# Re-ordering the seams of a two-block transformer kernel: weight splits on GpSimd, matmuls of one half first, modulation segments hosted elsewhere

## The reference, cut to what matters

```python
def ada_norm(x, g, shift, scale):
    return rms_norm(x, g) * (1.0 + scale) + shift

def swiglu(h, w_in, w_out):
    a, b = jnp.split(h @ w_in, 2, axis=-1)
    return (jax.nn.silu(a) * b) @ w_out

for l in range(DEPTH):
    mx = (s_lat @ ada_w[l] + ada_b[l]).reshape(bsz, N_MOD, 1, d)
    x = x + 0.5 * mx[:, 2] * swiglu(ada_norm(x, norm_g[l, 0], mx[:, 0], mx[:, 1]), ffn_w_in[l, 0], ffn_w_out[l, 0])
    hx = ada_norm(x, norm_g[l, 1], mx[:, 3], mx[:, 4])
    ...   # even or odd mixer on hx (and the context), giving yx
    x = x + mx[:, 5] * yx
    x = x + 0.5 * mx[:, 8] * swiglu(ada_norm(x, norm_g[l, 2], mx[:, 6], mx[:, 7]), ffn_w_in[l, 1], ffn_w_out[l, 1])
```

## Time and profile before

| quantity | value |
|---|---|
| median of 3 runs | 2415.8 us (2412.93 to 2417.66) |
| the profiled execution's own time | 2415.8 us |
| its span, first to last instruction | 2414.0 us |
| TensorE matmul busy | 2302.7 us, 95% |
| VectorE, ScalarE, GpSimd busy | 1156.8, 855.3, 154.4 us |
| mean granted TensorE clock | 0.978 |

### The profile page before, as it was taken

How to read it: one execution, slowest core, us unless ns; L and a number is a source line. 1 busy time by engine, 2 the same in 40 slices (tenths; PEclk the granted TensorE clock), 3 DMA queues, 4 the chain that set the end, 5 groups by cost and what they waited for, 6 DMA issues and landing times.

```text
span 2414.0 us, 36092 instructions
## 1 busy us (share of the span) xinstructions
PE 2302.7 (95%) x13748; PEld 1881.9 (78%) x13748; DVE 1156.8 (48%) x1955; ACT 855.3 (35%) x1388; POOL 154.4 (6%) x137
## 2 busy tenths in 40 slices
PE   6999999999999999978899999999999999988998
PEld 4777797877777788856787777788888876967998
DVE  5226375643433444475553333354343345566665
ACT  4125454632212232246432222233222234355544
POOL 0003112100000010040100000010000010000000
PEclk8999999999999999998999999999999998998999
DMA  9653543445555354300355665343243232323574
GB/s 299 195 161 95 166 139 87 145 127 172 180 179 175 89 146 140 114 10 27 96 154 149 189 188 149 111 123 88 70 118 90 79 104 70 88 70 113 164 205 119
DMA packets 514693, 313.01 MB, mean 130 GB/s; under 512 B 15899, under 2 KB 513138, under 8 KB 514454
## 3 DMA queue, kind: packets, MB, share of 16 engines
q1 hardware_dynamic: 513992, 311.33, 44.1%
q10 hardware_dynamic: 590, 0.16, 0.0%
HBM read 310.41 MB, written 1.05 MB: 129 GB/s over the span
## 4 chain that ended last, share of the span: by engine, by line
PE 85%; DVE 8%; ACT 3%; issue 2%; DMA 1%; ACTq 0%; POOL 0%; DVEq 0%; POOLq 0%
PE ps L1033 64%; PE ps L1075 4%; PE ps L768 4%; PE ps L982 2%; DVE w_lo L1814 2%; ACT w_hi L1351 1%; PE ps L2067 1%; PE ps L952 1%; PE ps L910 1%; PE ps L2388 1%; PE ps L2046 1%; PE ps L879 1%; PE ps L2054 1%; PE ps L841 1%; PE ps L2368 1%
## 5 line engine op out<-in xcount | busy, mean ns | idle before, releaser
L1033 PE MATMUL ps<-h_hi,w_hi 128*128 128x512 f32 (+1 forms) x2096 | 758.4, 362 | 20.7 <-DVE w_lo L1814 9.0
L1033 PE MATMUL ps<-h_hi,w_lo 128*128 128x512 f32 (+1 forms) x2096 | 746.2, 356 | 0.0
L1033 PE MATMUL ps<-h_lo,w_hi 128*128 128x512 f32 (+1 forms) x2096 | 746.2, 356 | 0.0
L1033 PEld LDWEIGHTS ps<-h_hi,w_hi 128*128 128x128 f32 x2096 | 397.9, 190 | 109.9 <-issue 36.8
L1814 DVE TENSOR_TENSOR w_lo<-stage,w_hi 128x1024 fp32r<-128x1024 f32 x227 | 283.2, 1250 | 393.5 <-ACT w_hi L1351 393.2
L1033 PEld LDWEIGHTS ps<-h_hi,w_lo 128*128 128x128 f32 x2096 | 398.3, 190 | 62.4
L1033 PEld LDWEIGHTS ps<-h_lo,w_hi 128*128 128x128 f32 x2096 | 398.4, 190 | 58.7
L1351 ACT ACTIVATE w_hi<-stage 128x1024 fp32r<-128x1024 f32 x227 | 236.7, 1055 | 364.8 <-PE ps L1033 251.0
L1814 DVE TENSOR_TENSOR w_lo<-deep,w_hi 128x1024 fp32r<-128x1024 f32 x184 | 224.9, 1232 | 266.7 <-ACT w_hi L1351 265.7
L1351 ACT ACTIVATE w_hi<-deep 128x1024 fp32r<-128x1024 f32 x184 | 190.7, 1054 | 171.0 <-PE ps L1033 121.0
L1033 PE MATMUL ps<-g_hi,w_hi 128*128 128x512 f32 (+1 forms) x660 | 242.6, 368 | 0.5 <-DVE w_lo L1814 0.2
(11 more groups left out here) (404 smaller groups left out, 2825.9 us busy)
## 6 DMA issues: line engine op xcount, KB each, us to landing
modw<-in_ada_w SPq DMA_DIRECT2D x72, 1024.0 KB, 6.1
stage<-in_ffn_w_in SPq DMA_DIRECT2D x88, 512.0 KB, 4.9
deep<-in_ffn_w_in SPq DMA_DIRECT2D x88, 512.0 KB, 4.0
modw<-in_w_mod SPq DMA_DIRECT2D x18, 1024.0 KB, 7.8
stage<-in_w_in SPq DMA_DIRECT2D x30, 512.0 KB, 4.8
stage<-in_ffn_w_out SPq DMA_DIRECT2D x32, 384.0 KB, 3.5
stage<-in_even_w_in SPq DMA_DIRECT2D x24, 512.0 KB, 4.0
deep<-in_ffn_w_out SPq DMA_DIRECT2D x32, 384.0 KB, 3.6
```

Source lines behind the costliest of these rows:

```text
L1033: last = mm(ps[:, j, 0:b - a], w_part[wp][:, u % RING, c, :], x_part[xp][:, x, a:b], start=first and wp == xp, stop=final and wp == "lo")
```

## The change

It has five parts.

1. Seams A and B host no modulation segments any more (`segs` is gone, in the plan and in all engines' code). The four segments go to the two gemms at L301 and L305, which follow seam A; each of them now hosts four segments (`hper=4`) and not two.
2. TensorE's order `behind` for v=0 becomes (0,0) to (0,4), then (1,0), (0,5), (1,1), (0,6), (1,2), (0,7), then (1,3) to (1,7). The sums of the second half move to after (0,5), its `pe_half_rstd` to after (0,7).
3. GpSimd makes two of the w_lo tiles in each seam: u0+5 and u0+7 in A and C, with its second `add` between them, and u0+4 and u0+5 in B, with the second `add` behind both. DVE makes u0+4 as before and u0+6 ahead of chunk 5's `low` in A and C, and none in B between the chunks. DVE waits on `w_ready` there, so that the count keeps its order.
4. ACT's splits are spread: one each ahead of `high` of chunks 0, 1, 2 and 3 in A and C, and ahead of chunks 1 and 3 in B. Its root for the second half comes behind all eight `high`.
5. On DVE `low` of chunk c now stands ahead of `scaled` of chunk c+1 for v=0, and the diagonal of the second half comes behind all eight chunks.

```diff
-            seam(tail, w, (0, 1), dst=0, segs=2)
+            seam(tail, w, (0, 1), dst=0)
...
-            gemm(w, 512, 4, "copy", dst=4, hper=2)
+            gemm(w, 512, 4, "copy", dst=4, hper=4)
...
-            gemm(w, 1536, 4, "copy", dst=8, hper=2)
+            gemm(w, 1536, 4, "copy", dst=8, hper=4)
...
-            behind = [(q, n) for ns in (chunks[:2], chunks[2:3], *([n] for n in chunks[3:])) for q in range(2) for n in ns]
+            behind = [(0, n) for n in chunks[:5]] + [(q, n + 5 * (1 - q)) for n in chunks[:3] for q in (1, 0)] + [(1, n) for n in chunks[3:]]
...
-            return ((4,), (5, 6), (7,)) if len(p.kw["ks"]) == 2 else ((), (4,), (5,))
+            return (((4,), (5,), (6,), (7,)), (5, 7)) if len(p.kw["ks"]) == 2 else (((), (4,), (), (5,)), (4, 5))
...
             for c in range(KC):
-                for s in seam_splits(p)[c] if c < 3 else ():
-                    dve_split(eng, u0 + s)
+                if c == 0 and per == 2:
+                    dve_split(eng, u0 + 4)
+                if c == 5 and per == 2:
+                    eng.wait_ge(S("w_ready"), u0 + 6)
+                    dve_split(eng, u0 + 6)
                 if c in (0, 2):
                     evacuate(1, c // 2)
+                low(0, c)
                 if c + 1 < KC:
                     scaled(0, c + 1)
-                low(0, c)
-                if c == 6:
-                    dve_half_diag(eng, p, 1, 2)
+            dve_half_diag(eng, p, 1, 2)
             scaled(1, 0)
...
+            def split(u):
+                eng.wait_ge(S("w_hi"), u + 1)
+                eng.wait_ge(S("w_ready"), u)
+                up(nc.gpsimd.tensor_tensor(w_lo[:, u % RING], arrival(u)[0], w_hi[:, u % RING].bitcast(F32), ALU.subtract), "w_ready")
+
             add(0)
-            add(1)
+            split(u0 + first)
+            if first == 5:
+                add(1)
+            split(u0 + second)
+            if first == 4:
+                add(1)
```

More of the change, by code:

```diff
@@ L247, in plan, with seam @@
         last = l == DEPTH - 1
-        def seam(tail, start, norm, dst=None, segs=0):
+        def seam(tail, start, norm, dst=None):
             units = 2 * len(tail["ks"]) + 4
@@ L254, in seam @@
                 r.update({"x_done": 4, "sg_half": 4, "gh_hi": 4, "g_half": 2, "g_ready": 2})
[L255 to L259, removed]
+            add("seam", r, start=start, norm=norm, dst=dst, **tail)
         def ffn(i, nt, hpers, after=None):
@@ L316, in plan @@
             gemm(("even_w_out_2", 0), 0, KC - 2, "resid", sumsq="early", **tail)
-            seam(dict(w=("even_w_out_2", 0), **tail), ("ffn_w_in_2", 0, 1), (0, 2), segs=2)
+            seam(dict(w=("even_w_out_2", 0), **tail), ("ffn_w_in_2", 0, 1), (0, 2))
         else:
@@ L987, in pe_seam @@
                         up(last, "unit_done", by=2) if v else up(last, "x_done")
[L988 to L992, removed]
+                    if v == 0 and (q, n) == (0, 5):
                         early_sums(1)
                         sums(1)
-                    if v == 0 and (q, n) == (1, 5):
+                    if v == 0 and (q, n) == (0, 7):
                         pe_half_rstd(eng, p, 1, 2)
@@ L1302, in act_seam @@
             for c in range(KC):
-                for s in seam_splits(p)[c] if c < 3 else ():
-                    act_split(eng, u0 + s)
+                if c < 4:
+                    for s in seam_splits(p)[0][c]:
+                        act_split(eng, u0 + s)
                 high(0, c)
@@ L1752, in dve_seam @@
             for c in range(KC):
-                for s in seam_splits(p)[c] if c < 3 else ():
-                    dve_split(eng, u0 + s)
+                if c == 0 and per == 2:
[3 more added lines that the diff above has]
+                    dve_split(eng, u0 + 6)
                 if c in (0, 2):
                     evacuate(1, c // 2)
+                low(0, c)
                 if c + 1 < KC:
                     scaled(0, c + 1)
-                low(0, c)
-                if c == 6:
-                    dve_half_diag(eng, p, 1, 2)
+            dve_half_diag(eng, p, 1, 2)
             scaled(1, 0)
-            if k["segs"]:
-                dve_rows(eng, p, 0, 2, 1, 1)
             for c in range(KC):
@@ L1770, in dve_seam @@
                     gated(0, c // 7)
-                if c == 5 and k["segs"]:
-                    dve_cols(eng, p, 0, 2, 1, 1)
+            eng.wait_ge(S("w_ready"), u1 + 4)
             dve_split(eng, u1 + 4)
@@ L1929, in pool_seam @@
         def pool_seam(eng, p):
+            u0 = p.at("unit_done")
+            first, second = seam_splits(p)[1]
             def add(v):
```

4 lines of the change are left out of this document (1 added, 3 removed).

## The result

The changed kernel takes 2442.07 us (median of 4 runs, 2437.34 to 2444.86), the kernel before 2416.73 us beside it: a ratio of 1.0105, 95% interval 1.0085 to 1.0127, or 20 to 31 us more. The forecast was 2437 us, range 2423 to 2447. Slower is right, and the time is 5 us above the likeliest value.

A forecast was written before the change was run, and what follows sets the result against it. TensorE was taken as the bound, its matmuls filling 95% of the span. Seams 13.3, moved segments 5.3 and clock 2.5 us sum to +21.1 us on 2415.8: 2437 us, range 2423 to 2447.

The forecast's parts named there:

- the sum of the seams: New parts of seams A, B and C together: +13.3 us from the layouts, and 2.5 for the clock.
- The chunk cycle: DVE and ACT in v=0 of the seams: 1.44 us per chunk, TensorE waiting about 0.74 us for chunks 1 to 4.
- GpSimd's split: One w_lo tile of 1024 columns on GpSimd in the seams takes 2.40 us, bounds 1.29 and 3.61.
- Blocking: In the seams DVE's low waits until GpSimd's split ends; seams cost 13.3 us with this, 5.0 without.
- Rival 1: GpSimd and DVE don't block each other in the seams: seams +5.0 us, total 2426 us; chance 0.20.
- Seam A: New part +3.9 us: tile 7's late DMA and GpSimd's split delay the chunks, w_lo 7 coming after 12.8 us.
- Seam B: New part +4.1 us: GpSimd's tiles 4 and 5 block low of chunks 1 and 3.
- Seam C: New part +5.3 us: v=0 ends 5.9 later, waiting for GpSimd's tile 7; the second wait shrinks by 0.7.
- Clock: TensorE, partly idle, drops to the 1.2 GHz level in all three seams: +2.5 us, bounds 0 and 7.
- The segments: Gemms behind seam A: four moved segments at 1.1 us plus 0.1 refill, two transpose pairs at 0.25: +5.3 us.
- Rival 2 (collision): Segment DMAs collide in gemms with four segments: plus 3 to 6 us on 2437, 2441 us; chance 0.13.
- Rival 3 (faster): h_lo 1 to 4 run ahead of TensorE, leaving no wait in the new parts: -7.6 us, 2408 us; chance 0.03.

The follow-up runs named there:

- order_only: Changed kernel with all undone but TensorE's v=0 order, the places of sums and roots, and the spread of ACT's and DVE's splits: 1.0019 times the kernel before.
- gpsimd_only: Kernel before with only GpSimd's two splits per seam, their waits and DVE's tile 6 as in the changed kernel: 1.0050 times the kernel before.
- gates_late: Kernel before with silu and gated of the first tile pair behind chunk 7, not 4, in v=1 of seams B and C: 0.9977 times before.
- low_first_only: Kernel before with only DVE's low of chunk c put ahead of scaled of chunk c+1 in v=0: 0.9994 times the kernel before.
- pool_one_input: Changed kernel with GpSimd's two splits per seam made one-input instructions (w_hi times zero), leaving out those tiles' low part: 2429.78 us, one run.
- segs_moved_only: Kernel before with only the four segments moved from seams A and B into the two gemms behind seam A: 1.0025 times the kernel before.
- dve_splits: Changed kernel with GpSimd's two splits per seam given back to DVE, low still ahead of scaled: 1.0060 times the kernel before.
- scaled_ahead: Changed kernel with DVE's scaled of chunk c+1 again ahead of low of chunk c in v=0: 1.0073 times the kernel before.

## Why the prediction was right, step by step

The pair of profiled executions is 29.85 us apart. The new parts have 15.05 of it, the two gemms with four segments 6.26, the old parts ahead of them -0.72. The other 9.3 lie where the change moves nothing: 2.96 before seam A, 2.7 between the two gemms and seam B, 3.6 behind seam C (there the changed kernel's matmuls run at the slower of two rates, shown in the last section). order_only has 2.0 and 4.4 us at the last two places, though its instructions there are those of before; gpsimd_only and gates_late start seam A earlier than before. The prediction had no term for this spread; by medians the kernel is 25.3 us slower, and the terms that can be placed give 20.6, just inside the interval of 20 to 31.

The mechanism was right: the signs that the prediction named are in the trace, but for two in seam A, its longest wait (below) and its length of 35.25 us for about 33. That the sum of the seams came out so close (15.05 against 15.8) is partly luck. The layouts had `low` freed too late, which made seams B and C 1.5 and 1.0 us too long, and the term for the clock was too small by 2.1.

- **The chunk cycle, 1.44 us**: measured 1.45 (1643.91 to 1645.36). TensorE's steps for chunks 3 and 4 of seam A start 1.45 us apart too (897.78 and 899.23); the trace shows 0.49 us of it as idle where 0.74 was told, since it counts a matmul as busy beyond the start of the next. low_first_only shows for the old order what the prediction says of chunks 5 to 7: with two steps of TensorE per chunk the cycle is covered. It costs only under the new order.
- **GpSimd's split, 2.40 us**: 2.38.
- **Blocking**: `low` at 2.31 us beside it. Rival 1 (no blocking, 2426 us) falls by this row. But the prediction's price for blocking, 8.3 us (13.3 less 5.0), is not shown: pool_one_input, with almost none, has seams only 3.3 us shorter than the changed kernel. Its GpSimd instructions are 0.4 us longer and its clock in C is lower, so the 3.3 is no exact price either.
- **Seam A, +3.9**: +5.32. Tile 7 is ready 12.7 us after the part's start, as laid out (12.8). From there to the end it is 22.5 us, not 20.2. TensorE is busy throughout that stretch, at a clock of 0.86: the missing 2.3 us are put down to the clock, which no experiment changed by itself. TensorE's longest wait in A is not where the prediction had it: it stands before chunk 3 (3.15 us), and the wait for GpSimd's tile 7 is 1.60.
- **Seam B, +4.1**: +3.99, with two errors that cancel. The longest wait stands before chunk 3 as told, 2.48 us. But h_lo 3 is ready 7.3 us after the start, 1.5 earlier than laid out (8.85), mostly since `low` of chunk 3 did not have to wait for GpSimd's `add`. From there to v=1 it is 12.7 us and not 11.1, with a low clock in it that the layout did not have (0.79):

```profile
1231.40:1239.40 8.00, 7.16 (x46) 6.96 (x47) 4.39 (x11) 2.29 (x5) 0.88 (x2) 0.79 0.63 197
```

- **Seam C, +5.3**: +5.74. Tile 7 comes 10.5 us after the start, 1.0 earlier than laid out, because the blocked `low` got its turn before GpSimd's `add` did (rows above: `low` ends at 1640.88, `add` takes 0.93 and not 0.74). The 22.7 us behind it, at a clock of 0.92, were laid out as 21.2.
- **Clock, +2.5**: what lies over the layouts behind the last late tile or chunk is 2.3 us in A, 1.6 in B and 1.5 in C, 5.4 in all. Of this the prediction took 0.8 as the slow stretch that seam A had before, so the term comes to 4.6, an estimate from these three differences. It was sized too small.
- **The segments, +5.3**: 6.26. The term that was too small is the transposes: 0.25 us a pair counts no wait, as in a gemm with two segments, where DVE's sum is long done. With four, the transposes of the first pair follow the rows at once and wait 0.55 us, and transposes and wait together cost 0.9 a pair.
- **Rival 2 (collision)**: SP does hold the third and fourth segments back (12.77 us for the two DMAs in its queue), but no wait of TensorE for modw follows.
- **Rival 3 (faster)**: no part of the change, alone or with others, was faster than before by more than can be measured.

Each part alone gives 6.0 (segments), 12.1 (GpSimd), -1.5 (low first, not clear of zero) and 4.6 us (order with spread), 21.2 in all; the whole gives 25.3, and its interval reaches down to 20. So the totals prove no effect of the parts on each other.

What stays open: whether the 25.3 us of the medians exceed the 20.6 that have a place at all, whether scaled ahead of low is worth 3 or 8 us, what the blocking is worth in seams A and C, and what holds `low` for 0.5 us beside a one-input instruction.

## What to carry to other kernels

A helper engine that takes work off a busy one can be paid for twice, if it is slower at it (2.38 against 1.22 us here) and shuts the other out meanwhile (2.31 us for a `low` of 0.48): look at whether the next instruction of the relieved engine has the operands that collide, and at when the helper's last piece is needed. An order in which the consumer asks for one input per step needs the producers' cycle at or below the step; the same cycle is free if the consumer alternates with work that it already has. Before work is moved out of a place that looks crowded, check whether the new place has idle time: a filler that hides half its cost in waits pays all of it in a dense loop.

## What the runs showed of the hardware

- ACT's silu brings a table load of 1.28 us with it; it, the silu and three instructions of `gated` in the middle of the chunk chain cost TensorE waits of 1.41 us in B and 1.51 in C of the kernel before.
- Late in the kernel the same 128x256 matmuls run at two rates under the same granted clock of 1.00: a spacing of 0.113 us (91 records in 10 us) in before, or 0.118 (87) in the changed kernel, order_only and segs_moved_only. The same stretch takes 87.0 us in before (2279.5 to 2366.5) and 90.5 in the changed kernel (2306.0 to 2396.4), which makes 3.5 of the 3.6 us behind seam C. dve_splits, gpsimd_only and scaled_ahead have the faster rate there, gates_late the slower one, so it does not go with the change; with one trace for each kernel, no run tells whether it differs from one execution to the next. Before, and then after:

```profile
2340.00:2350.00 10.00, 10.00 (x91) 10.00 (x89) 5.93 (x9) 3.80 (x7) 0.00 (x0) 1.00 0.72 202
```

```profile
2370.00:2380.00 10.00, 10.00 (x87) 10.00 (x86) 5.51 (x10) 4.67 (x6) 0.00 (x0) 1.00 0.60 173
```

- A one-input GpSimd instruction of 128x1024 took 2.77 us, more than the two-input subtraction (2.38); DVE's subtraction of this size took 1.22.
